# Norms between the parts of a layer, worked in token halves and partly under the last weight unit

## The reference, cut to what matters

```
h = h + 0.5 * rms_norm(swiglu(rms_norm(h, ng[0]), w_in0, w_out0), ng[1])
u = rms_norm(h, ng[2])
out, ... = mixer(u, ...)
h = h + rms_norm(out, ng[3])
h = h + 0.5 * rms_norm(swiglu(rms_norm(h, ng[4]), w_in1, w_out1), ng[5])
```

## Time and profile before

| | |
|---|---|
| time of the runs | 2822.31 us median of 3 (2821.88 to 2825.8) |
| profiled execution | span 2825.6 us from first to last instruction; its own time is not listed beside it |
| PE busy | 2623.7 us, 93% |
| DVE, ACT, POOL busy | 40%, 31%, 37% |
| mean granted PE clock | 0.962 of full speed |
| HBM traffic | 71 GB/s over the span |

### The profile page before, as it was taken

The page is one execution under the profiler, slowest core; times in us unless marked ns, Lnnn a source line. Parts: engine busy times, 40 slices in busy tenths (PEclk is TensorE's granted clock), DMA queues, the critical chain, the costliest instruction groups (busy, mean ns, idle before and its releaser), DMA issues. The chain is left out here.

```text
span 2825.6 us, 61605 instructions
## 1 busy us (share of the span) xinstructions
PE 2623.7 (93%) x26993; PEld 2540.6 (90%) x26993; DVE 1124.5 (40%) x1382; ACT 880.2 (31%) x1223; POOL 1056.0 (37%) x495
## 2 busy tenths in 40 slices
PE   7999998997999999999999999799588888999997
PEld 7999998996888899999899999799377858999997
DVE  3333117845544433321433311631654454433312
ACT  4222223233323422222322222333523333322221
POOL 3444442333434344443344443133034353244432
PEclk9999999998998999999999999899789999999999
DMA  4223221221012222322222222122000022122221
GB/s 149 82 89 99 92 74 60 87 67 38 2 61 105 68 89 82 94 93 81 62 88 89 92 92 85 32 89 73 19 3 3 4 81 81 53 89 89 99 88 46
DMA packets 53585, 202.82 MB, mean 72 GB/s; under 512 B 6320, under 2 KB 6448, under 8 KB 53424
## 3 DMA queue, kind: packets, MB, share of 16 engines
q1 hardware_dynamic: 53424, 200.38, 21.7%
HBM read 190.68 MB, written 9.67 MB: 71 GB/s over the span
## 5 line engine op out<-in xcount | busy, mean ns | idle before, releaser
L302 POOL TENSOR_TENSOR wlo<-raw,whi 128x1024 fp32r<-128x1024 f32 (+1 forms) x261 | 708.8, 2716 | 1124.8 <-ACT whi L277 1124.8
L332 PE MATMUL ps<-xh,whi 128*128 128x272 f32 x3600 | 1039.5, 289 | 6.6 <-POOL wlo L302 3.2
L334 PE MATMUL ps<-xh,wlo 128*128 128x272 f32 x3600 | 1043.5, 290 | 0.0
L333 PE MATMUL ps<-xl,whi 128*128 128x272 f32 x3600 | 1036.0, 288 | 0.0
L332 PEld LDWEIGHTS ps<-xh,whi 128*128 128x128 f32 x3600 | 678.6, 189 | 9.8 <-issue 5.8
L333 PEld LDWEIGHTS ps<-xl,whi 128*128 128x128 f32 x3600 | 679.5, 189 | 0.0
L334 PEld LDWEIGHTS ps<-xh,wlo 128*128 128x128 f32 x3600 | 677.4, 188 | 0.0
L277 ACT ACTIVATE whi<-raw 128x1024 fp32r<-128x1024 f32 (+1 forms) x261 | 297.7, 1140 | 1128.3 <-PE ps L334 1108.4
L334 PE MATMUL ps<-mh,wlo 128*128 128x272 f32 x1408 | 406.1, 288 | 0.0
L333 PE MATMUL ps<-ml,whi 128*128 128x272 f32 x1408 | 405.4, 288 | 0.0
L332 PE MATMUL ps<-mh,whi 128*128 128x272 f32 x1408 | 405.0, 288 | 0.0
(11 more groups left out here) (470 smaller groups left out, 3295.2 us busy)
## 6 DMA issues: line engine op xcount, KB each, us to landing
raw<-w SPq DMA_DIRECT2D x245, 512.0 KB, 3.5
raw<-w SPq DMA_DIRECT2D x64, 704.0 KB, 4.1
mS<-state_gdn SPq DMA_DIRECT2D x8, 512.0 KB, 5.0
gdn_s_s<-mS SPq DMA_DIRECT2D x8, 512.0 KB, 2.8
h<-xT SPq DMA_DIRECT2D x4, 544.0 KB, 8.0
yT<-h SPq DMA_DIRECT2D x4, 544.0 KB, 2.7
go_r<-w SPq DMA_DIRECT2D x4, 512.0 KB, 5.6
S<-state_rwkv SPq DMA_DIRECT2D x8, 256.0 KB, 4.1
```

Source lines behind the costliest of these rows:

```text
L302: pool.tensor_tensor(wlo[two][:, 0:kt * P], raw[slot][:, 0:kt * P], whi[two][:, 0:kt * P].bitcast(F32), ALU.subtract).then_inc(w_lo, 1)
L332: pe.matmul(o, wh, hi[:, r, :], start=(start and k == 0), stop=False)
L333: pe.matmul(o, wh, lo[:, r, :], start=False, stop=False)
L334: mm = pe.matmul(o, wl, hi[:, r, :], start=False, stop=(stop and k == kt - 1))
```

## The change

The turns are worked in token halves. In the last unit of an output product the first half's result is squared, summed and its root spread while PE runs the second half: `unit_mm` gets `inserts`, calls that stand ahead of an input tile of the second half (the sums at k = 2, the spread at k = 9 for a FFN and 7 for the others). DVE walks 16 half tiles, with the reciprocal of the second half's root behind the fourth. PE takes the first three units half by half, 9 matmuls a half tile. The squares for the next norm are no longer summed on PE for each tile: POOL adds them, 6 additions of 272 columns a half, and PE sums twice at the end. The fourth unit's high and low parts stand between the halves. The spread of norm q + 1 stands behind the first half of unit 3 instead of ahead of the unit. The output products of GDN and RWKV use three PSUM pairs in turn instead of four. At the start, the wait for the constants stands behind the tiles, and DVE adds the squares of norm 0. At the end, the output is stored in five pieces of a half each instead of four pieces of two tiles. In the fourth turn, the subtraction for the carried rows (`shift_low_dve`) stands behind the norm instead of ahead of it.

The core of the diff (the renamed counts of the semaphores and the calls are left out):

```diff
+        def unit_mm(pe, name, u, j, out, hi, lo, k0=0, start=True, stop=True, inserts=None, halves=(0, 1)):
 
             base, kt = BASE[name], KT[name]
             n = base + u + j
             two = (base + j) % 2
             pe.wait_ge(w_lo, n + 1)
-            for half in range(2):
+            for half in halves:
                 for k in range(kt):
-                    if ready is not None and half == 0:
-                        pe.wait_ge(x_lo, ready + k + 1)
+                    if inserts is not None and half == 1 and k in inserts:
+                        inserts[k]()
...
+            unit_behind_norm(pe, name, q)
+
+        def unit_behind_norm(pe, name, q):
+            unit_mm(pe, name, 0, 3, pair(3), xh, xl, halves=(0,))
             spread_norm_pe(pe, q)
-            unit_mm(pe, name, 0, 3, pair(3), xh, xl)
+            unit_mm(pe, name, 0, 3, pair(3), xh, xl, halves=(1,))
 
         def behind_norm_tiles(pe, name, q):
 
-            base = BASE[name]
+            base, e = BASE[name], q // 2 - 1
             bufs = [(EARLY[name][0][j], EARLY[name][1][j]) for j in range(2)] + [(whi[base % 2], wlo[base % 2])]
-            for k in range(NM):
-                pe.wait_ge(x_lo, 8 * SETS[name] + k + 1)
-                for j in range(3):
-                    if k == 0:
-                        pe.wait_ge(w_lo, base + j + 1)
-                    if j == 1:
-                        square_sum_pe(pe, q, k)
-                    first_products(pe, j, k, *bufs[j], halves=(0, 1) if j < 2 else (0,))
-            if q:
-                pe.wait_ge(h_upd, 8 * (q // 2))
-
-        def behind_norm_half(pe, name):
-            two = BASE[name] % 2
-            for k in range(NM):
-                first_products(pe, 2, k, whi[two], wlo[two], halves=(1,))
+            if q == 0:
+                for k in range(NM):
+                    pe.wait_ge(x_lo, 8 * SETS[name] + k + 1)
+                    for j in range(3):
+                        if k == 0:
+                            pe.wait_ge(w_lo, base + j + 1)
+                        first_products(pe, j, k, *bufs[j])
+                pe.wait_ge(mf_in, 16)
+                pe.wait_ge(sq_added, 6)
+                pe.wait_ge(sq_ready, 8)
+                quarter_sums(pe, norm_bank(q), tb[2], True, False)
+                quarter_sums(pe, norm_bank(q), tb[1], False, True).then_inc(sq_added, 1)
+                return
+            for half in range(2):
+                for k in range(NM):
+                    pe.wait_ge(xl_half, 16 * e + 8 * half + k + 1)
+                    for j in range(3):
+                        if k == 0 and half == 0:
+                            pe.wait_ge(w_lo, base + j + 1)
+                            pe.wait_ge(sq_ready, sq_base(q - 1) + 7)
+                        if k == 0 and j == 1:
+                            pe.wait_ge(y_half, 2 * e + half + 1)
+                        first_products(pe, j, k, *bufs[j], halves=(half,))
+                    if half == 0 and k == 0:
+                        half_sums_pe(pe, q - 1, 1)
+                    if half == 0 and k == 3:
+                        spread_half_pe(pe, q - 1, 1)
+            pe.wait_ge(sq_pool, 12 * (e + 1))
+            pe.wait_ge(sq_half, 16 * (e + 1))
+            quarter_sums(pe, norm_bank(q), tb[2], True, False)
+            quarter_sums(pe, norm_bank(q), tb[1], False, True).then_inc(sq_rows, 1)
+            pe.wait_ge(h_upd, 16 * (e + 1))
...
+        def half_sums_pe(pe, q, half):
+            if half == 0:
+                pe.wait_ge(sq_added, added_base(q) + 7)
+            pe.wait_ge(sq_ready, sq_base(q) + 8 + half)
+            quarter_sums(pe, 6 + half, tb[2], True, False, (2 * half, 2 * half + 1))
+            quarter_sums(pe, 6 + half, tb[1], False, True, (2 * half, 2 * half + 1)).then_inc(sq_added, 1)
+
+        def spread_half_pe(pe, q, half):
+            pe.wait_ge(rs_ready, roots_before(q) + half + 1)
+            r = rows_of(half)
+            for qd in (2 * half, 2 * half + 1):
+                mm = pe.matmul(post_row(half)[:, QT * (qd % 2):QT * (qd % 2) + QT],
+                               M["ident"][r, 32 * qd:32 * qd + 1].broadcast_to([64, P]), rs[r, 0, 0:QT], start=True, stop=True)
+            mm.then_inc(nrm_mm, 1)
...
+        def turn_act(act, q, then, between=None):
+
+            def part(half, m):
+                e = q // 2 - 1
+                act.wait_ge(h_upd, 16 * e + 8 * half + m + 1)
+                act.activation(xh[:, 2 * m + half, :], h[:, 2 * m + half, :], ACT.Copy,
+                               scale=v(V_NORM + q * NM + m)).then_inc(xh_half, 1)
+                if m > 2:
+                    act.wait_ge(sq_pool, 12 * e + 6 * half + m - 2)
+                act.activation(tb[m % 2 if m else 2][:, half, :], h[:, 2 * m + half, :], ACT.Square).then_inc(sq_half, 1)
+            part(0, 0)
+            part(0, 1)
+            half_root_act(act, q - 1, 1)
+            for m in range(2, NM):
+                part(0, m)
+            early_hi(act, then, 3)
+            if between is not None:
+                between()
+            for m in range(NM):
+                part(1, m)
             norm_act(act, q)
-            if sett is None:
-                norm_copy_act(act, q)
-
-        def pre_norm_low(dve, q, sett, m):
-
-            dve.wait_ge(x_hi, 8 * sett + m + 1)
-            dve.scalar_tensor_tensor(xl[:, 2 * m:2 * m + 2, :], h[:, 2 * m:2 * m + 2, :], v(V_NORM + q * NM + m),
-                                     xh[:, 2 * m:2 * m + 2, :].bitcast(F32), ALU.mult, ALU.subtract).then_inc(x_lo, 1)
-
-        def post_norm_dve(dve, q, step, sett=None, y=y):
-
-            root_dve(dve, q)
-            dve.wait_ge(nrm_mm, q + 1)
-            base = 8 * (q // 2)
-            for m in range(NM):
-                if base + m > 0:
-                    dve.wait_ge(h_upd, base + m)
-                dve.tensor_tensor(tb[3][:, :, :], y[:, 2 * m:2 * m + 2, :], post_rows(), ALU.mult).then_inc(h_tmp, 1)
-                if sett is not None and m:
-                    pre_norm_low(dve, q + 1, sett, m - 1)
-                dve.wait_ge(h_tmp, base + m + 1)
-                dve.scalar_tensor_tensor(h[:, 2 * m:2 * m + 2, :], tb[3][:, :, :], step,
-                                         h[:, 2 * m:2 * m + 2, :], ALU.mult, ALU.add).then_inc(h_upd, 1)
-            if sett is not None:
-                pre_norm_low(dve, q + 1, sett, NM - 1)
+
+        def half_squares_pool(pool, q, half):
+            e = q // 2 - 1
+            for m in range(1, NM - 1):
+                pool.wait_ge(sq_half, 16 * e + 8 * half + m + 1)
+                if m > 1:
+                    pool.wait_ge(sq_pool, 12 * e + 6 * half + m - 1)
+                pool.tensor_tensor(tb[2][:, half, :], tb[2][:, half, :], tb[m % 2][:, half, :], ALU.add).then_inc(sq_pool, 1)
+
+        def turn_pool(pool, name, q):
+            for j in range(3):
+                early_lo(pool, name, j)
+            half_squares_pool(pool, q, 0)
+            early_lo(pool, name, 3)
+            half_squares_pool(pool, q, 1)
+
+        def pre_norm_low(dve, q, half, m):
+
+            dve.wait_ge(xh_half, 16 * (q // 2 - 1) + 8 * half + m + 1)
+            dve.scalar_tensor_tensor(xl[:, 2 * m + half, :], h[:, 2 * m + half, :], v(V_NORM + q * NM + m),
+                                     xh[:, 2 * m + half, :].bitcast(F32), ALU.mult, ALU.subtract).then_inc(xl_half, 1)
+
+        def post_norm_dve(dve, q, step, last=False, y=y):
+
+            base = 16 * (q // 2)
+            half_root_dve(dve, q, 0)
+            for n in range(2 * NM):
+                half, m = n // NM, n % NM
+                if m == 0:
+                    dve.wait_ge(nrm_mm, roots_before(q) + half + 1)
+                if base + n > 1:
+                    dve.wait_ge(h_upd, base + n - 1)
+                if m == NM - 1:
+                    dve.wait_ge(y_half, 2 * (q // 2) + half + 1)
+                t = tb[3][:, m % 2, :]
+                dve.tensor_tensor(t, y[:, 2 * m + half, :], post_row(half), ALU.mult).then_inc(h_tmp, 1)
+                if n and not last:
+                    pre_norm_low(dve, q + 1, (n - 1) // NM, (n - 1) % NM)
+                dve.wait_ge(h_tmp, base + n + 1)
+                dve.scalar_tensor_tensor(h[:, 2 * m + half, :], t, step, h[:, 2 * m + half, :], ALU.mult, ALU.add).then_inc(h_upd, 1)
+                if n == 3:
+                    half_root_dve(dve, q, 1)
+            if not last:
+                pre_norm_low(dve, q + 1, 1, NM - 1)
...
```

`last_tile` on ACT, `ahead_of_end` and the order in `out_pe`:

```diff
+            def last_tile(n):
+                act.wait_ge(sq_added, added_base(q) + NM - 2)
+                for half in range(2):
+                    act.wait_ge(acc, 2 * n + 1 + half)
+                    act.activation(tb[1][:, half, :], pair(1)[:, half, :], ACT.Square).then_inc(sq_ready, 1)
+                    act.activation(y[:, 2 * NM - 2 + half, :], pair(1)[:, half, :], ACT.Copy, scale=v(V_NORM + q * NM + NM - 1)).then_inc(y_half, 1)
+                    if half == 0:
```

(18 more changed lines are left out.)

198 lines of the change are left out of this document (101 added, 97 removed).

## The result

| | before | changed |
|---|---|---|
| time of the runs | 2823.5 us median of 4 | 2846.8 us median of 4 (2843.4 to 2849.25) |
| ratio | | 1.0073, 95% interval [1.0059, 1.0087] |
| profiled execution | span 2825.6 us | span 2847.5 us |
| mean granted PE clock | 0.962 | 0.962 |

The changed kernel is slower by 20.6 us (the ratio on 2823.5); 2830 had been forecast, with a range to 2838. A second set of five runs gave 1.0071 [1.0058, 1.0084] (experiment e9). GpSimd gets in between and holds the half update, as forecast, but the rounds that this gives were priced too low, two waits of ScalarE were missing, and the start gained less than forecast.

A forecast was written before the change was run, and what follows sets the result against it. TensorE, busy 93% of the span, was taken to bound the kernel. Turns +15.1, start -6.8, first FFN +1.2 and end -1.2 make +8.3 us on the median 2822.31: 2830.6, rounded to 2830, range 2801 to 2838.

The forecast's parts named there:

- H, the first half update: End of a turn's first updated half tile of h: 5.53 us behind the first half's end, at 421.6 us.
- Who goes first: In a turn, GpSimd's addition gets in ahead of VectorE's half update: chance 0.53, 2830 us, own range 2820 to 2840.
- The round: In a turn, one half tile's h, xh, xl, h: 1.93 us with GpSimd in between, 1.43 if not.
- Turns: The five stretches from last product to next norm's spread: +15.1 us in sum with GpSimd in between, -11.4 if not.
- The spread's 3.0: Moved behind half a unit, the spread comes 3.0 us later, taken in full in the first and fourth turn.
- The FFN entries' wait for the sixth unit: In front of four FFNs, TensorE waits for the sixth unit's low part: 1.2 us lost each, 0 to 1.9.
- its +0.6: The fourth turn takes 0.6 us more with GpSimd in between, 4.7 less if not.
- GpSimd's price: GpSimd getting in between in the five turns or not: +15.1 us against -11.4.
- The bracket's 24.6: Fifteen rounds of the first turn if GpSimd does not get in: 24.6 us, against 29.9 if it does.
- Start: No wait for constants, fewer sums: -6.8 us, +1.2 for the first FFN; a first product later than 12 us refutes it.
- End: Last norm and output: h ends near 2821.8 for 2822.48, smaller last transfer, -1.2 us.
- The clock: Rival: TensorE, in use for only 1.2 of every 1.93 us in the turns, gets a lower clock; chance 0.05.

The follow-up runs named there:

- e9: The changed kernel once more, nothing edited, for more runs and a second trace: 2845.8 us, ratio 1.0071.
- e10: The changed kernel with GpSimd's addition of a tile waiting for that tile's low part (xl) on VectorE: 2816.9 us, ratio 0.997.
- e1: The changed kernel with GpSimd's addition of a tile waiting for the next tile's half update of h: 2821.9 us, ratio 0.9988.
- e5: The kernel before with only the change's first norm (start): 2819.1 us, ratio 0.9976.
- e14: All the combined edits, additions released by the low part, and ScalarE's second-half root one half tile later, against the kernel before: 2793.6 us, ratio 0.9881.
- e6: The changed kernel with ScalarE copying the first high part ahead of the last tile's second half, behind FFNs only: 2840.3 us, ratio 1.0049.
- e4: The changed kernel with the following norm's row spread before the fourth unit's first half, as in the kernel before: 2845.6 us, ratio 1.0067.
- e7: The changed kernel with each GpSimd addition of squares taking one column and not 272, only to price them: 2814.1 us, ratio 0.9961.
- e8: The changed kernel with later additions, VectorE's late fourth low part, first high part copied earlier, and spread inside the fourth unit's first half: 2800.7 us, ratio 0.9905.
- e3: The changed kernel with the fourth unit's low part made by VectorE behind the turn, not by GpSimd: 2833.7 us, ratio 1.0028.
- e2: The changed kernel without GpSimd additions in the turns; TensorE sums each square by half tile, ScalarE has one more root: 2834.5 us, ratio 1.0026.

## Why the prediction failed, step by step

The forecast was that GpSimd gets in, and it did. What failed is the sum: a blocked round was put at 1.93 us and took 2.02, two waits of ScalarE stood at nothing, and the start was put at 5.6 us without the race that decides it.

- **H, the first half update: right.** 5.77 us behind the half's end (420.00 less 414.23) for 5.53.
- **Who goes first: right.** GpSimd asked 0.96 us after h for 0.96 to 1.05, against 1.01 for the next update, and went in ahead of 11 updates a turn, as forecast; the twelfth addition falls beside the reciprocal. Of the 80 half updates of the turns 57 lasted 0.9 us or more: these 55, and in the second and the fifth turn the first update, which GpSimd's low parts hold in e10 too. The margin was 0.05 us, so this could have gone otherwise; the prediction said so and gave it a chance of 0.53. The Trainium skill, page "SBUF — State Buffer", section "SBUF: two separate sides", says that of a VectorE instruction with two SBUF inputs and a GpSimd instruction that reads SBUF, whichever starts first gets the shared port pair for the whole instruction and the other fully blocks. e10 and e1 agree (an addition that asks 0.22 us behind the update waits it out). At the start the listed starts and the rule part by 0.03 us: VectorE was listed at 10.64 in e5, GpSimd at 10.67 with its plain 2.34, and GpSimd was in.
- **The round: the term that was too small.** 2.02 for 1.93. I had the addition hold VectorE off for 0.55 from xl's end, with no reason given and below the 0.636 that the earlier trace rows give for 256 columns; it ends at 1.73 after h, 0.65 from xl's end. Eleven rounds: 1.0 us a turn, 5.0 in five.
- **Two waits missing.** ScalarE runs its list in order. The first high part stood 0.67 us behind the last tile's second half, and the third behind the root that waits for TensorE (0.54). 29.9 + 1.0 + 0.67 + 0.54 = 32.1, the measured first turn. e14 shows the second wait, e6 the first (its first round is 1.44 us in all three turns). In five turns of the first trace the first wait costs 2.0 us and the second 1.3; in the second trace the second costs 5.6.
- **Turns.** 22.6 (and 26.7 in the second trace) for 15.1. The spread's 3.0 at the GDN and LoRA entries was wrong (e4: 0.9 and 0), and this hid the miss of 2.2 us in the rounds of the first turn: 3.9 for 3.6 in all, an agreement of two errors. The FFN entries' wait for the sixth unit came as 0.77 for 1.2. The fourth turn took 3.0 more than its +0.6: 1.8 of it are the rounds, and the half unit ahead of the spread, put at 3.0, took 5.0 at a granted clock of 0.58:
```profile
1818.46:1823.42 4.96, 4.96 (x26) 4.96 (x27) 0.00 (x0) 0.00 (x0) 0.00 (x0) 0.58 0.00 0
```
- **GpSimd's price: right in size.** +15.1 against -11.4, 26.5 us; e7 shows 27.0 us in the turns' lengths (157.9 less 130.9) and 32 in the ratios. Part of this is luck: the 55 blocked rounds cost 0.57 us each, 31 us in the turns, and the root's longer wait in the kernels without them gives 5 back. The bracket's 24.6 is also a slip, as 13 x 1.43 + 2.27 + 3.5 is 24.4.
- **Start: the race was missing.** The median of e5 has 6.8 for 5.6, but the traces show 1.8 at the end of the first FFN in the first and 5.0 in the second. The first product stood at 14.27 us in the first, and by the prediction's own sign (later than 12) its start is refuted; it holds where VectorE's low part is let in first. **End: -2.3** for -1.2.
- **The clock: not the cause, though its number fits.** That rival stood at 2845, beside the measured 2846.8. It wanted 1.2 GHz for whole turns; the first turn shows 0.90 (window 420.00 to 455.10) for 0.85 before. Short falls to 0.5 do cost time, through the root.
- **The sum.** The three terms of the first trace give 22.6 - 1.8 - 2.3 = 18.5 us, those of the second 26.7 - 5.0 - 2.3 = 19.4, for 20.6 by the ratio and 8.3 forecast. The turns missed by 7.5 and 11.6 us, the start by 3.8 and 0.6. The prediction gave a blocked round no bound above its estimate of 1.93, and its range ended at 2838, below the 2840 that it allowed this very case. The turns differ by 4 us between two executions of one kernel, and this is the root's wait in all five of them.

## What to carry to other kernels

When an instruction on GpSimd meets a chain on VectorE that reads two SBUF tensors, look at when it asks and not only at what it costs: here one more wait, which moved the request from 0.05 us ahead of the half update to 0.22 behind it, took away 27 us of the turns. Halving the tiles makes the pacing engine's round the bound, so every in-order wait of the feeding engine (a root for another norm, the last tile's copy) becomes part of it: list that engine's queue one instruction at a time, and where it waits for TensorE, price the wait at both levels of the clock. And give a derived duration its own error, above all if it is multiplied by sixty.

## What the runs showed of the hardware

- An exclusive hold between VectorE and GpSimd can be hidden entirely: twelve additions of some 0.65 us a turn under multiplications that read one operand from PSUM cost no more than additions of one column (e10 and e7, 26.5 us for the first turn in both).
- The same subtraction of 128x1024 takes VectorE 1.21 us (e8, e3: 1.22) and GpSimd 2.35 to 2.40.
- Two sums of 136 f32 columns with 32 output rows held TensorE for 0.44 us in e2, as long as three and a half products of 272 columns, and no less than four of them in the kernel before.
- The granted clock of one unchanged stage was 1.00 in two executions and 0.77 in a third of the same pair of kernels, worth 4.4 us; a single trace can put such a sum in the wrong place.
- A fall of TensorE's granted clock to 0.5 for 3 to 7 us reaches VectorE through ScalarE's order: the third low part waited 0.33 us at full clock and up to 1.80 with such a fall, in turns with the same code (the changed kernel's two traces).
